# High and low weights of a block back to back, instead of sixteen high products and then sixteen low ones

## The reference, cut to what matters

```python
D_MODEL = 2048; SEQ = 256; DEPTH = 2; D_FF = 4 * D_MODEL

for l in range(DEPTH):                                   # first block
    mod = c_act @ w_ada[l] + b_ada[l]                    # vector only, done on VectorE
    h = rms_norm(x, g_pre_mix[l]) * (1.0 + scale_a) + shift_a
    y = token_mixer(h, w_in[l], ..., w_out[l])           # h @ w_in, mixers, [hm, ha] @ w_out
    x = x + gate_a * rms_norm(y, g_post_mix[l])
    h = rms_norm(x, g_pre_mlp[l]) * (1.0 + scale_m) + shift_m
    y = jnp.square(jax.nn.relu(h @ w_up[l])) @ w_down[l]
    x = x + gate_m * rms_norm(y, g_post_mlp[l])

uz = rmsnorm(h, g_pre) @ w_in                            # second block, layer 0 (S5)
y = jax.nn.gelu(s5_ssm(u, ...)); y = y * sigmoid(y @ w_glu + b_glu)
h = h + rmsnorm((y * silu(z)) @ w_out, g_post)
kvf = rmsnorm(h, g_kv) @ w_kv                            # second block, layer 1 (attention)
qz = rmsnorm(h, g_pre) @ w_in
h = h + rmsnorm((fox_attention(q, k, v, cum) * silu(z)) @ w_out, g_post)
```

## Time and profile before

| | |
|---|---|
| device time, 3 runs | 3263.88, 3269.46, 3270.71 us; median 3269.46 us |
| profiled execution | span 3265.3 us, 49414 instructions |
| granted TensorE clock, mean | 0.980 of full speed |
| TensorE busy | 3117.1 us, 95% of the span |
| VectorE busy | 2510.6 us, 77% |
| ScalarE busy | 1569.2 us, 48% |
| memory read | 769.28 MB, 241 GB/s over the span |

### The profile page before, as it was taken

The page is one execution under the profiler, slowest core; times in us unless marked ns, Lnnn a source line. Parts: engine busy times, 40 slices in busy tenths (PEclk is TensorE's granted clock), DMA queues, the critical chain, the costliest instruction groups (busy, mean ns, idle before and its releaser), DMA issues. The chain is left out here.

```text
span 3265.3 us, 49414 instructions
## 1 busy us (share of the span) xinstructions
PE 3117.1 (95%) x20322; PEld 2698.4 (83%) x20322; DVE 2510.6 (77%) x3120; ACT 1569.2 (48%) x2327; POOL 0.2 (0%) x4
## 2 busy tenths in 40 slices
PE   4899999999999999999999999999998999999998
PEld 3788878888888878888888888887886888888887
DVE  7997999798888787777887566788569677556665
ACT  2455654344444556765444444445443455333454
POOL 0000000000000000000000000000000000000000
PEclk7999999999999999999999999999999999999999
DMA  9777859888888645553687666775655554554353
GB/s 409 301 306 302 316 228 353 334 334 339 335 337 328 232 180 194 217 209 129 259 327 263 228 229 206 268 259 207 225 173 181 181 182 142 207 181 146 139 184 112
DMA packets 136976, 790.24 MB, mean 242 GB/s; under 512 B 20081, under 2 KB 38897, under 8 KB 46001
## 3 DMA queue, kind: packets, MB, share of 16 engines
q1 hardware_dynamic: 108002, 754.65, 62.1%
q10 hardware_dynamic: 28752, 32.45, 3.0%
HBM read 769.28 MB, written 17.76 MB: 241 GB/s over the span
## 5 line engine op out<-in xcount | busy, mean ns | idle before, releaser
L1518 DVE TENSOR_TENSOR wl<-raw,wh 128x2048 fp32r<-128x2048 f32 x479 | 1096.4, 2289 | 244.1 <-ACT wh L874 243.4
L394 PE MATMUL bk<-HX,wh 128*128 128x512 f32 x4592 | 1113.2, 395 | 2.9 <-ACT wh L874 1.6
L394 PEld LDWEIGHTS bk<-HX,wh 128*128 128x128 f32 x4592 | 842.4, 188 | 176.7 <-ACT wh L874 2.7
L874 ACT ACTIVATE wh<-raw 128x2048 fp32r<-128x2048 f32 x479 | 913.6, 1908 | 33.5 <-DMA raw<-in_w_in 26.4
L394 PEld LDWEIGHTS bk<-HX,wl 128*128 128x128 f32 x4592 | 571.4, 188 | 29.3 <-DVE wl L1518 6.5
L394 PE MATMUL bk<-HX,wl 128*128 128x256 f32 x4592 | 578.8, 278 | 2.6 <-DVE wl L1518 2.6
L394 PE MATMUL bk<-hb,wh 128*128 128x512 f32 x2048 | 494.1, 393 | 5.5 <-ACT hb L874 5.0
L1526 DVE SCALAR_TENSOR_TENSOR raw<-raw,cb 128x2048 f32<-128x2048 f32 x192 | 437.1, 2283 | 13.9 <-DMA raw<-in_w_ada 13.9
L394 PEld LDWEIGHTS bk<-hb,wh 128*128 128x128 f32 x2048 | 376.6, 188 | 82.2 <-ACT hb L874 5.8
L394 PEld LDWEIGHTS bk<-hb,wl 128*128 128x128 f32 x2048 | 256.4, 189 | 12.3 <-DVE wl L1518 1.8
L394 PE MATMUL bk<-hb,wl 128*128 128x256 f32 x2048 | 258.9, 279 | 0.9 <-DVE wl L1518 0.9
(11 more groups left out here) (276 smaller groups left out, 2690.6 us busy)
## 6 DMA issues: line engine op xcount, KB each, us to landing
raw<-in_w_ada SPq DMA_DIRECT2D x192, 1024.0 KB, 6.1
raw<-in_w_up SPq DMA_DIRECT2D x128, 1024.0 KB, 5.2
raw<-in_w_down SPq DMA_DIRECT2D x128, 1024.0 KB, 5.1
raw<-in_w_in SPq DMA_DIRECT2D x68, 1024.0 KB, 5.1
raw<-in_kv_w SPq DMA_DIRECT2D x33, 1024.0 KB, 4.8
raw<-in_w_out SPq DMA_DIRECT2D x32, 1024.0 KB, 4.8
raw<-in_s_w_in SPq DMA_DIRECT2D x32, 1024.0 KB, 4.9
raw<-in_fox_w_in SPq DMA_DIRECT2D x32, 1024.0 KB, 4.7
```

Source lines behind the costliest of these rows:

```text
L394: return e.matmul(o_, l_, r_, start=start, stop=stop, skip_group_check=True)
L874: return e.activation(o_, i_, f, **kw)
L1518: return e.tensor_tensor(o_, a_, b_, op)
```

## The change

In `slab` the loop over the low weights is merged into the loop over the high weights: after the 512-column product of block k with WH comes at once the 256-column product of the same block with WL. The wait for s_free, which stood behind sixteen high products, now stands behind one. Number, shape and operands of the products are the same, and so is their bank. `first_out` is left as it is, so 477 of the 479 split slabs change.

```diff
@@ -407,8 +407,8 @@
                     if first:
                         first(k)
                     mm(bank[:, :], WH[w][:, k, :], x(k).rearrange("p a t -> p (a t)"), q == 0, False)
-                e.wait_ge(s_free, FREE_AT[POS[j]])
-                for q, k in enumerate(order):
+                    if q == 0:
+                        e.wait_ge(s_free, FREE_AT[POS[j]])
                     last = mm(bank[:, 0:T], WL[w][:, k, :], x(k)[:, 0, :], False, q == KT - 1)
                 last.then_inc(s_slab, 1)
```

## The result

| | before | after |
|---|---|---|
| device time, median of 4 runs each | 3269.54 us (3263.88 to 3270.71) | 3366.17 us (3364.22 to 3373.76) |
| profiled execution | span 3265.3 us | 3365.62 us, span 3363.7 us |
| granted TensorE clock, mean | 0.980 | 0.982 |

The ratio is 1.0302 [1.029, 1.0314]: the change costs 3.0%. The span grew by 98.3 us, where the forecast was 70 (3340 us). The measured 3366 us lie inside the forecast range of 3300 to 3375 us, near its upper end.

The account below looks back on a forecast made before the run. TensorE, busy 95% of the span, was taken as the bound. Stage waits of 29 + 11 + 16 + 5 + 6.5 + 4, less 2 gained, made 70 us; pairs added none: 3340 us, range 3300 to 3375.

Parts of the forecast that it names:

- The wait that moves: All stages: low weights needed 0.23 us into the slab, not 3.66, so late subtractions stall TensorE; bounds 55 to 95 us, chance 0.73.
- the gain at awaited slabs: Slabs whose activation blocks are awaited one by one: low products fill TensorE's wait, -2 us in all.
- Every second slab of a late run pays: Late slabs: VectorE's chain hangs on the end of slab n-1, so full lateness is paid alternately; 29 us in layer 0's MLP.
- The MLP of layer 1: 41 late slabs, 32 us if paid in full; half taken, 16, in case ScalarE and VectorE take the shift back.
- The products themselves: All 7632 high-low pairs on TensorE: 0.345 us each, no change, with 15 us kept on each side.
- The bounds of that step: Pair time under long alternation: 100 us gained if products reach plain float32 speed, 60 us lost if low products slow likewise.
- the rival of quicker alternation: All 7632 pairs 13 ns shorter, weight load hidden under the longer product: 100 us, giving 3240 us; chance 0.04.
- Paid once per stage: VectorE's idle time takes the shift up, so each stage pays only its largest lateness: some 20 us, 3290; chance 0.12.
- Paid in full: Every lateness in every stage costs its whole length: 105 to 110 us, 3380 us; chance 0.09.
- Nothing happens: All lateness hides under TensorE's existing 25 waits for low weights (15.8 us): 3269 us; chance 0.02.

Follow-up runs that it names:

- experiment 1: Kernel before, old order of products, but TensorE waits for the low weights after the first high product: 3326.65 us, ratio 1.0171.
- experiments 11 and 12: Kernel before with 160 modulation tiles shortened to about half (results wrong): old wait 3260.51 us; wait after the first high product 3288.96 us.
- experiments 2 and 3: Low products read WH, wait for low weights ahead of the slab's last product (results wrong): first in pairs, 3302.77 us; second in the old order, 3267.62 us.
- experiment 9: Kernel before, but in slabs awaiting activations block by block the last four blocks go in high-low pairs: 3264.80 us against 3266.91, ratio 0.9989.

## Why the prediction was right, and where it was short

- **The wait that moves: right in mechanism, and 13 us too large.** 70 us were forecast (72 without the gain at awaited slabs, which experiment 1 can't have), 57 measured with the wait alone (experiment 1), near the lower end of 55 to 95. By stage, forecast and measured there: MLP of layer 0, 29 and 30.9; projections and w_out of layer 0, 11 and 13.4; the same of layer 1, 6.5 and 9.2; S5 z, 5 and 3.5; the later stages 4 and -2 (with the unexplained -3.9 between S5's z and its gated unit in it). "Every second slab of a late run pays" is shown by the timelines of both kernels, and by experiments 11 and 12 to hang on VectorE's chain. Of the 57 waits forecast in the MLP of layer 0 the change has 50, 27.1 us in all, by the list of waits of the weight loads (PEld). One sign missed: in w_out of layer 0 the even period was to stay 6.1 us, and it went from 6.14 to 6.27.
- **The MLP of layer 1: too large.** 16 us forecast, with a lower bound of 8; 1.7 measured in experiment 1. In experiment 1 its shift against the kernel before was 53 us at the start, 58 by the end of the first up-projection, then 54 behind the first down slab, where the waits for activations (the earlier trace rows show one of 2.13 us) took 4.2 back. Over the nine slabs around, where ScalarE and VectorE are held by set-up work for S5, the shift fell from 53.3 to 51.0 us instead of rising by 2.2 a slab, and only the last slabs added 4.2. I had named this condition and then taken half of the sum instead of following it.
- **"The products themselves": this step failed.** "So I take 0.345 us a pair, no change" rested on the passages from high to low and back in the old order, one each in a slab. They don't price alternation at every product: pairs take 348.9 or 353.3 ns, groups of two 345.0, groups of four 345.8. 7632 pairs by 4.1 to 8.5 ns are 31 to 65 us, and 59 us by the mean of 7.7; measured are 35 (medians) to 45 us (spans) in experiments 2 and 3. Where VectorE sets the pace slower pairs only fill a wait: w_out of layer 0 didn't grow in experiment 2 (-1.7 us). My range had 15 us for this term.
- **The bounds of that step: a misread row, and luck.** The 160 records of the earlier trace rows aren't 160 products. They are five slabs of 16 products, two records to each. One such slab before:

```profile
204.08 7.07 PE L394 MATMUL bk<-hf,raw 128*128 128x256 f32 x32
210.99 0.38 PE L398 MATMUL bk<-cst,ta 128*128 128x128 f32 x2
```

16 plain float32 products take 6.91 us, 0.432 us each or 0.216 a record, where a split product of as many columns takes 0.116. So the fp32r products aren't slower than the float32 ones, as the rival of quicker alternation supposed, and the 0.221 us, to which the ends of the last products had been added, is half a product. The upper bound of 8 ns a pair, or 60 us, came near the measured 4.1 to 8.5 by luck: with 0.216 in place of 0.221 the same reasoning gives 13 ns.
- **The sum** was 28 us short because of this term, and less than the term itself because the waits had been put 13 us too high. Waits alone (56.7) and order alone (45.5) give 102 us of span; the change took 98.3. By medians it is 58 and 35 against 97. They add up nearly in full. In the MLP of layer 0 they don't: 30.9 and 17.0 alone, 38.2 together. A longer slab gives VectorE more time: the latenesses over 0.23 us add up to 31.8 us there in experiment 1 and to 27.5 in the change.
- **That 3366 us lie in the range is partly luck.** Its upper part was meant for 95 us of waits and 10 for the pairs. What filled it was 57 us of waits and 35 to 45 for the pairs.
- **The rival of quicker alternation** went the other way. The Trainium skill's formula for the isolated gap (TensorE: Matmul & The Clock Gate, "Back-to-back issue gap") would make a pair 325 ns; none of the stretches read here came below 344.8.
- **Paid once per stage** holds where VectorE is saturated: w_out of layer 0 grew by 1.8 us in experiment 1. **Paid in full** would have been 40 us in the MLP of layer 0 and 32 in that of layer 1, against 30.9 and 1.7. **Nothing happens** fell with the 98 us.
- **The gain at awaited slabs** was there in experiment 9, 3.2 us at the one I named, where I had put "up to 3 us". In the change it wasn't made at that slab. From its start to the next work it took 9.7 us before (1628.96 to 1638.66), 5.7 in the change (1699.15 to 1704.81), and 5.5 in experiment 1 (1687.15 to 1692.70), where no low product fills anything: TensorE was 58 to 70 us behind by then, the activations were less so, and no wait was left to fill. At the first slab of the S5 output the new order does gain: 7.32 us before, 7.31 in experiment 1, 6.37 in the change.

What stays open is why TensorE is slower when lengths alternate, and what picks one of the two paces. Weight tile, repeated activations and bank columns are excluded by runs (for the weight tile with equal lengths and for the bank's columns, one run of each kernel). That weight loads interact with the lengths of the products on both sides is left, but no run tested it.

## What to carry to other kernels

When a consumer is moved ahead of its old place, compare the producer's finish with the new need slab by slab, and follow a late one through the loop by which the producer itself waits: here it cost its lateness every second time, and nothing where another engine set the pace. A passage that a trace shows once in sixteen products doesn't price one that comes at every product: put a range on it and use its middle. Here groups of two kept the old pace of the products, though not the old time, since their early wait stayed. Count how many records a product has before a row's mean is taken for a product. Low products pay as filling only where the high ones wait for activations, so put them there and leave the rest in sixteens.

## What the runs showed of the hardware

- Products of 512 and 256 columns that take turns one by one take 348.9 or 353.3 ns a pair, at a granted clock of 1.00 and with no idle time, where the same products in groups of two, four or sixteen take 345.0, 345.8 and 344.8. Both products are slower: in the ten slabs of the key and value stage the mean steps went from 229.2 and 115.6 ns to 234.0 and 119.3, in those of the gated unit to 230.0 and 118.9.
- Two weight tiles that take turns with equal lengths cost next to nothing: 229.5 against 229.0 ns a product of 512 columns.
- A plain float32 product of 256 columns has two records of 0.216 us and takes 0.432 us (16 of them in 6.91 us), against 0.116 for an fp32r one.
- After a wait for low weights the waiting product starts 0.05 to 0.06 us after VectorE's subtraction ends, and its own step is 0.10 to 0.11 us longer: over 95 such waits in the change and 97 in experiment 1, as in the earlier trace rows.
